# One expert weight slab fetched by a wide transfer and sixteen transfers of eight partitions

## The reference

```python
def ec_moe(u, w_router, w_gate, w_up, w_down):     # 16 experts, cap = 32 tokens each
    aff = softmax(u @ w_router)
    gates, idx = top_k(swapaxes(aff, 1, 2), cap)   # every expert chooses its tokens
    xs = u[bidx, idx]
    hid = silu(einsum('becd,edf->becf', xs, w_gate)) * einsum('becd,edf->becf', xs, w_up)
    ys = einsum('becf,efd->becd', hid, w_down) * gates[..., None]
    return zeros_like(u).at[bidx, idx].add(ys)
```

## Time and profile before

| | |
|---|---|
| median of the runs | 2803.36 us |
| the profiled execution | 2800.74 us |
| its span, first to last instruction | 2798.9 us |
| PE busy | 2359.4 us (84%) |
| DVE busy | 1194.0 us (43%) |
| ACT busy | 511.5 us (18%) |
| moved by DMA | 691.38 MB, mean 247 GB/s |

### The profile page before, as it was taken

The page is one execution under the profiler, slowest core; times in us unless marked ns, Lnnn a source line. Parts: engine busy times, 40 slices in busy tenths (PEclk is TensorE's granted clock), DMA queues, the critical chain, the costliest instruction groups (busy, mean ns, idle before and its releaser), DMA issues.

```text
span 2798.9 us, 45220 instructions
## 1 busy us (share of the span) xinstructions
PE 2359.4 (84%) x19823; PEld 1842.4 (66%) x19823; DVE 1194.0 (43%) x2238; ACT 511.5 (18%) x1143; POOL 189.9 (7%) x322
## 2 busy tenths in 40 slices
PE   7999987555655655555899999999999999999999
PEld 4676763111211221111699988999999998899999
DVE  2555632000000000000466667774665666776565
ACT  4444421000000000000210125411011012451200
POOL 0363610000000000000000001000000000100000
PEclk9999989888888887878999999999999999999999
DMA  7534449999999999999644354344454444434443
GB/s 259 159 102 134 136 151 419 425 426 429 427 427 428 427 428 428 427 428 427 236 163 173 133 174 167 132 172 157 169 178 153 172 173 161 145 133 168 164 155 117
DMA packets 212625, 691.38 MB, mean 247 GB/s; under 512 B 36876, under 2 KB 76237, under 8 KB 186829
## 3 DMA queue, kind: packets, MB, share of 16 engines
q1 hardware_dynamic: 204685, 683.74, 63.4%
q10 hardware_dynamic: 7744, 4.75, 0.6%
HBM read 684.23 MB, written 4.23 MB: 246 GB/s over the span
## 4 chain that ended last, share of the span: by engine, by line
PE 61%; DMA 30%; DVE 4%; ACT 2%; SPq 1%; issue 1%; ACTq 0%; DVEq 0%
PE bank L1942 18%; DMA slab_ring<-in_moe_w_up 14%; PE bank L1990 10%; DMA slab_ring<-in_moe_w_down 8%; PE bank L2192 7%; PE bank L401 5%; PE bank L2285 4%; DMA slab_ring_more<-in_moe_w_up 3%; PE bank L2033 3%; PE bank L1909 3%; PE bank L1420 2%; DMA slab_ring_more<-in_moe_w_down 2%; PE bank L2088 1%; DMA slab_ring_more<-in_moe_w_gate 1%; PE bank L2168 1%
## 5 line engine op out<-in xcount | busy, mean ns | idle before, releaser
L1420 PE MATMUL bank<-slab_ring,chosen_xT 128*32 128x512 f32 x1248 | 194.1, 756 | 136.7 <-DMA slab_ring<-in_moe_w_up 73.8
L1942 PE MATMUL bank<-slab_ring 128*128 128x128 f32 x2560 | 299.0, 275 | 0.4 <-ACT lru_gelu L2399 0.4
L1942 PEld LDWEIGHTS bank<-slab_ring 128*128 128x128 f32 x2560 | 292.3, 192 | 0.5 <-issue 0.5
L1577 DVE TENSOR_TENSOR beaten_then_hidden<-bank,beaten_then_hidden 128x512 f32<-128x512 f32 x16 | 11.1, 691 | 559.5 <-PE bank L1420 559.5
L1942 PE MATMUL bank<-layer_uT,slab_ring 128*128 128x128 f32 x1920 | 227.5, 275 | 0.0
L1420 PEld LDWEIGHTS bank<-slab_ring,chosen_xT 128*32 128x32 f32 x1248 | 38.2, 124 | 281.0 <-DMA slab_ring<-in_moe_w_up 116.2
L1942 PEld LDWEIGHTS bank<-layer_uT,slab_ring 128*128 128x128 f32 x1920 | 221.1, 192 | 0.2
L1420 PE MATMUL bank<-slab_ring_more,chosen_xT 128*32 128x512 f32 x800 | 130.0, 783 | 93.4 <-DMA slab_ring_more<-in_moe_w_up 47.7
L1990 PE MATMUL bank<-slab_ring 128*128 128x128 f32 x1408 | 165.7, 275 | 0.0
L1990 PEld LDWEIGHTS bank<-slab_ring 128*128 128x128 f32 x1408 | 161.4, 192 | 0.0
L1420 PEld LDWEIGHTS bank<-slab_ring_more,chosen_xT 128*32 128x32 f32 x800 | 25.1, 127 | 193.3 <-DMA slab_ring_more<-in_moe_w_up 78.5
(11 more groups left out here) (476 smaller groups left out, 3687.3 us busy)
## 6 DMA issues: line engine op xcount, KB each, us to landing
slab_ring<-in_w_up SPq DMA_DIRECT2D x44, 2048.0 KB, 7.9
slab_ring<-in_moe_w_up SPq DMA_DIRECT2D x39, 2048.0 KB, 46.2
slab_ring<-in_moe_w_gate SPq DMA_DIRECT2D x39, 2048.0 KB, 45.8
slab_ring<-in_moe_w_down SPq DMA_DIRECT2D x38, 2048.0 KB, 46.2
slab_ring<-in_w_in SPq DMA_DIRECT2D x28, 2048.0 KB, 8.2
slab_ring_more<-in_moe_w_down SPq DMA_DIRECT2D x26, 2048.0 KB, 46.7
slab_ring_more<-in_moe_w_gate SPq DMA_DIRECT2D x25, 2048.0 KB, 45.4
slab_ring_more<-in_moe_w_up SPq DMA_DIRECT2D x25, 2048.0 KB, 46.3
```

Of the source, the lines that this page charges most:

```text
L1420: ins = nc.tensor.matmul(out[32 * c:32 * c + 32, 0:cols], x, slot_of((q * EXPERT_SLABS + i) % NRE).rearrange("p (k n) -> p k n", k=2 if co ...
L1577: nc.vector.tensor_tensor(hid, ps[1][:, :], sg, ALU.mult).then_inc(ex.next("hidden"), 1)
L1942: i = nc.tensor.matmul(out[:, j * P:(j + 1) * P], a[:, k, j * P:(j + 1) * P], x[:, k, :], start=(start and j == 0 and k == 0), stop=(k == ...
```

## The change

Slab 96 (expert 8, first gate slab, slot 6) is no longer one transfer. Its first 1536 values of every partition still come by one transfer over all 128 partitions, which raises the slot's semaphore. The other 2560 values of every partition come by 16 transfers, each of which covers eight neighbouring partitions. These raise a semaphore of their own, and TensorE waits for all 16 of them before it touches the slab. The bytes, their places in SBUF and the other 191 slabs are as before.

```diff
+NARROW_SLAB = 8 * EXPERT_SLABS
+NARROW_FROM = 1536
...
+    s_narrow = ctx.enter_context(nc.semaphore("narrow_slab_loaded"))
...
                 if n >= NRE:
                     sp.wait_ge(env.slab_free, freed(0, n - NRE + 1))
                 src = expert_slab(env, e, i)
-                sp.dma_start(slot_of(n % NRE).rearrange("p (k n) -> p k n", k=src.shape[1]), src).then_inc(env.full[n % NRE], 16)
+                if n == NARROW_SLAB:
+                    flat = src.rearrange("p r n -> p (r n)")
+                    sp.dma_start(slot_of(n % NRE)[:, 0:NARROW_FROM], flat[:, 0:NARROW_FROM]).then_inc(env.full[n % NRE], 16)
+                    for p in range(0, P, 8):
+                        sp.dma_start(slot_of(n % NRE)[p:p + 8, NARROW_FROM:], flat[p:p + 8, NARROW_FROM:]).then_inc(s_narrow, 16)
+                else:
+                    sp.dma_start(slot_of(n % NRE).rearrange("p (k n) -> p k n", k=src.shape[1]), src).then_inc(env.full[n % NRE], 16)
...
                 pe.wait_ge(env.full[n % NRE], 16 * ((n % NRE < EARLY_MOD) + n // NRE + 1))
+                if n == NARROW_SLAB:
+                    pe.wait_ge(s_narrow, 16 * P // 8)
```

## The result

The changed kernel takes 2814.14 us, the median of five runs (2813.82 to 2815.82), beside 2803.44 us for the kernel before in the same series (five runs, 2802.49 to 2806.33). The ratio is 1.0039 with a 95% interval of 1.0028 to 1.0050: 10.7 us slower. The forecast was 2812.8 and slower.

A forecast was written before the change was run, and what follows sets the result against it. The experts were taken as bound by the DMA engines moving weights, the second block by PE. Slab 96 costs eight engines 1.85 + 12.3 + 0.14 = 14.3 us instead of 4.90: +9.4 on 2803.36 gives 2812.8 us, range 2805 to 2826.

The forecast's parts named there:

- The stage is bound by the DMA engines, and nothing gives the time back: Experts: weight slabs arrive 4.90 us apart; any delay on the slowest DMA engine reaches the second block's start in full.
- The cost is at the DMA engines' packets and no other place: Slab 96: added issues on SyncE and TensorE's added wait cost nothing; only the transfers' packets count.
- the prediction's cover: Queue ahead of slab 97: 46 us of work hides 40 us for 17 issues, leaving some 6 us.
- Eight engines carry the narrow part: Slab 96's eight-partition transfers: completion counts say only eight of 16 engines carry them, 6.16 us in all at full pace.
- Factor 2 and not 1, 4 or 8: Slowdown of slab 96's 385 ns narrow packets: factor 2, 770 ns, +9.4 us, chance 0.50; factor 8, +46.4 us, 0.02.
- abreast: Rival, factor 4: the eight engines reach each narrow transfer together, 1540 ns a packet, +21.7 us, 2825.1; chance 0.20.
- The other eight engines run ahead: Slab 96: engines without narrow packets spend 1.85 us instead of 4.90 and get 3 us ahead; nobody waits for them alone.
- The marks: Signs in the changed profile: 10.6 us idle before slab 96, start near 889, second block near 1364.7, DMA share dropping.
- Factor 1: Rival: narrow packets of slab 96 run at full pace, 385 ns, +3.2 us at most, 2806.6; chance 0.15 on the slowest engines.
- Hidden in the lead of others: Rival: the other eight engines are already up to 5.5 us late, so nothing is added, 2803.4; chance 0.08 including no effect.
- Starved queue: Rival: narrow issues on SyncE take 4.96 us each, 79 against 46 of queue; engines dry for 33 us, 2836; chance 0.04.

The follow-up runs named there:

- e3_wide16: Against the kernel before: four slabs' narrow values fetched by 16 transfers each over all 128 partitions, 160 values apiece; 2807.32 us beside 2802.69, ratio 1.0011.
- e10_near_half: Against the kernel before: on four slabs, narrow values of partitions 0 to 63 only, by eight transfers of eight neighbours; 2822.45 us beside 2803.15, ratio 1.0070.
- e9_own_half: Against the kernel before: on four slabs, narrow values of partitions 0 to 63 only, eight transfers of eight partitions four apart; 2802.11 us beside 2803.15, ratio 0.9995.
- e11_other_half: Against the kernel before: on four slabs, narrow values of partitions 64 to 127 only, eight transfers of eight partitions four apart; 2830.29 us beside 2803.15, ratio 1.0092.
- e7_halves: Against the kernel before: four slabs' narrow values fetched by two transfers of 64 neighbouring partitions each; 2838.82 us beside 2804.09, ratio 1.0120.
- e4_sixteen: Against the kernel before: four slabs' narrow values fetched by eight transfers of 16 neighbouring partitions each; 2835.48 us beside 2802.69, ratio 1.0108.
- e12: Against the kernel before: four slabs' narrow values fetched by four transfers of 32 neighbouring partitions each; 2837.47 us beside 2803.15, ratio 1.0122.
- e2_step4: Against the kernel before: four slabs' narrow values fetched by 16 transfers of eight partitions four apart; 2840.73 us beside 2802.69, ratio 1.0125.

## Why the prediction was right, step by step

*The stage is bound by the DMA engines, and nothing gives the time back.* Right. The second block starts later by 13.7 us in the traces and takes 1443 us as before.

*The cost is at the DMA engines' packets and no other place.* Right: 16 issues took 23.2 us instead of the 30 to 40 expected, and slab 97 landed 38.72 us after its issue, so the queue never ran out. e3_wide16 prices the issues, with the small packets' own overhead, at 1.2 us a slab. One slip stands in the prediction's cover: it took the whole 46 us from issue to landing for work ahead of slab 97, but 4.9 of them are the slab's own transfer. By its own 40 us for 17 issues the cover would have been 1 us and not 6; the faster issues made it ample.

*Eight engines carry the narrow part.* Right: the changed kernel has eight completions for each narrow transfer.

*Factor 2 and not 1, 4 or 8.* Right in size: 706 ns on average against 770 forecast, so the narrow part is 16 x 0.706 = 11.3 us, not 12.3. The reason given for it (the eight engines crowd on few partitions but don't stand abreast) fits the first half of the slab, in which the packets take 621 and 683 ns; abreast would have been 1540, and e10_near_half has 543 to 748 with nobody else there. For partitions 64 to 127 it is another: the lower eight engines write where the upper eight also write, and these two share. That is argued for the changed kernel, whose records can't part the two; the halves by themselves show it, 387 ns in e9_own_half and 773 in e11_other_half at slab 96. Nor does any record show why the eight don't stand abreast.

*The other eight engines run ahead.* This step failed. They were taken to be untouched and 3 us ahead; instead the full packets went from 613 to 1239 ns, and by the records of landings the first engine to finish slab 99 is 4.0 us late (with the 4.0 of before the change taken off), not 3 early. It did not spoil the sum, since nobody waits for them alone, but the same slowness also hits the lower eight engines before and behind their narrow packets. With the measured lengths the eight spend 16 x 0.706 + 8 x 0.325 (the wide part's packets, 325 ns on average in place of 231) + 0.14 - 4.90 = +9.1 us, and from slab 95 to slab 96 the matmuls' lateness does grow by 9.2, from 5.4 to 14.6. Slab 95 had added 1.4 by slower full packets, and 0.9 is gone again by slab 98, which leaves 9.7. The forecast's +9.4 is a slightly too long narrow packet set off against slow neighbours that it did not have. That the two nearly cancel is luck: in e7_halves the same kind of sum gives 3.3 us and the chip 8.7.

*The marks.* Idle time before slab 96: 8.95 us and not 10.6, because slab 95 was itself 1.4 us late and its matmuls took 1.4 us longer (3.37 us in place of 1.93); start at 894.53, which is 890.5 without the 4.0 us that this execution was late before, forecast 889. Second block at 1369.06, 1365.0 in the same way, forecast 1364.7. The slabs behind are 4.6 and 4.9 us apart. The DMA share was to drop between 872 and 890 and did not: 0.99 to 1.05. A stretched packet counts as busy; the mark should have been the rate, which fell from 418 to 223 GB/s.

*The rivals.* Abreast (+21.7) is refuted for this kernel by the packet lengths, and e4_sixteen, e7 and e12 never reach it either. Factor 1 is what e9_own_half shows, but only for partitions that the carrying engine writes in a full slab too. Hidden in the lead of others: no. The lead was small: in e9_own_half, where only the upper eight are relieved, the last engine of a slab comes 1.0 us earlier in the end, so the latest of the upper eight had been only that far behind the latest of the lower. Starved queue: no, though e3_wide16 came near it.

The Trainium skill has a rule for each of the two places. DMA: Bandwidth & Descriptors, section "The descriptor swizzle": in a transfer over all 128 partitions engines 0 to 7 write partitions 0 to 63 and 8 to 15 the rest, each engine one port, with four partitions and the four 32 further on. By it, eight partitions four apart below 64 put the lower eight engines each on its own port, if they take the rows in their order, and above 64 on the port of another engine. The traces agree, 387 ns in e9 and 773 in e11. Its page SBUF — State Buffer, section "Door 1: The DMA port swizzle (why `[64,N]` ≈ `[32,N]`)", says that 32 partitions reach as many ports as 64; e12 with +34.3 us and 194 GB/s and e7 with +34.7 and 202 to 206 agree. By that page's table 16 partitions should have half the rate of 32, and here they cost the same (e4 +32.8). The likely reason is that engines that stand at different transfers reach more ports between them than one transfer does; no run here separates that.

Neither rule says that engines on free ports are slowed. The page DMA: Bandwidth & Descriptors has, in "Back-pressure in remote DMA", that a saturated SBUF port clogs the path back to the source engines and to others that share it, which is told there of transfers between cores. e10 shows the like on one core: full packets at 930 ns on average, the upper engines' among them, beside a crowd that writes elsewhere.

## What to carry to other kernels

The stream of full-width transfers ran at its full 426 GB/s, and eight partitions four apart below 64 went along with it at no cost; both fit DMA engines that keep to partitions of their own. Large transfers over fewer partitions that break this order are dear: 8, 16, 32 or 64 neighbours cost 8 to 11 us per 1.31 MB here. It is neither the number of transfers nor that of engines that counts most, but where the engines write. If a slab must be cut, cut it along its values and keep all 128 partitions (1.2 us for 16 pieces). When a transfer's price is estimated, count the slower packets of its neighbours in the queue too, and watch GB/s rather than the DMA share.

## What the runs showed of the hardware that was not expected

- A crowded group of partitions slows engines that write elsewhere: 930 ns on average for full packets in e10_near_half between 880 and 883 us, in place of 614, with the share at 1.0.
- While the disturbance lasts, the total rate is about half of the usual 425 GB/s in most kernels: 223 and 235 in the changed kernel, 222 in e2_step4, 194 in e12_quarters, 202 and 206 in e7_halves, 226 in e11_other_half. In e10_near_half it is 257 and 291. Why engines that are back on full slabs stay slow while only a few narrow packets are left (in e2_step4, between 886 and 888 us, 22 full packets with a median of 1285 ns beside four of 10240 bytes) stays open.
- Packets of 640 bytes took 32 ns each, 20 GB/s an engine, where full ones reach 27: a cost of 1.0 us a slab.
